# A two-layer mixer and mixture-of-experts kernel: layer 1's modulation products placed in layer 0's merge, and half of layer 0's slot-token groups placed in the expert steps

## The reference

```python
mod = silu(c or c_ctx) @ w_mod[l] + b_mod[l]      # 6 x 1024: shift, scale, gate, twice
h   = rms_norm(x) * (1 + scale) + shift
p   = h @ w_in[l]                                 # q k v, pool, hyena, 3 x 1024 gates
y0, y1, y2 = neighbourhood_attention, multiscale_pool, hyena
x  += gate * (sum_n sigmoid(gates_n) * (y_n @ w_branch[l, n])) @ w_out[l]
h   = modulated rms_norm(x)
# router: 16 experts in 4 groups, best group, top 2 of it
out = sum_e gates[:, e] * ((silu(h @ w_gate[e]) * (h @ w_up[e])) @ w_down[e])
x  += gate * out
```

## Time and profile before

| What | Value |
|---|---|
| Median of 3 runs | 1738.56 us (1735.78 to 1742.26) |
| The profiled execution, its own time | 1740.76 us |
| Its span in the trace | 1739.0 us |
| PE busy | 1495.9 us (86%) |
| DVE busy | 850.8 us (49%) |
| ACT busy | 635.6 us (37%) |
| POOL busy | 368.8 us (21%) |
| DMA, mean over the span | 215 GB/s |

### The profile page before, as it was taken

The page is one execution under the profiler, slowest core; times in us unless marked ns, Lnnn a source line. Parts: engine busy times, 40 slices in busy tenths (PEclk is TensorE's granted clock), DMA queues, the critical chain, the costliest instruction groups (busy, mean ns, idle before and its releaser), DMA issues. The chain is left out here.

```text
span 1739.0 us, 19624 instructions
## 1 busy us (share of the span) xinstructions
PE 1495.9 (86%) x7748; PEld 1076.0 (62%) x7748; DVE 850.8 (49%) x1204; ACT 635.6 (37%) x848; POOL 368.8 (21%) x206
## 2 busy tenths in 40 slices
PE   6998998789999977999999787679889986977772
PEld 2465677568788746788888535468679973322322
DVE  4621765762223246899999556144764633100002
ACT  2422222372232242778777434223164441000003
POOL 0223222112233301111010122335226631000001
PEclk8999999899999986999999888889899997999996
DMA  8457221102232315899999772752314657999992
GB/s 298 170 194 274 74 73 49 36 11 73 92 126 72 121 32 226 343 401 406 406 400 400 252 262 85 294 202 97 100 43 152 206 203 293 420 420 423 422 375 85
DMA packets 120003, 374.32 MB, mean 215 GB/s; under 512 B 8270, under 2 KB 74000, under 8 KB 88944
## 3 DMA queue, kind: packets, MB, share of 16 engines
q1 hardware_dynamic: 109168, 334.58, 51.0%
q0 software_dynamic: 10752, 38.61, 5.9%
HBM read 356.39 MB, written 16.78 MB: 215 GB/s over the span
## 5 line engine op out<-in xcount | busy, mean ns | idle before, releaser
L658 POOL TENSOR_TENSOR w_lo<-ring,w_hi 128x1024 fp32r<-128x1024 f32 x120 | 299.2, 2503 | 629.3 <-ACT w_hi L1431 629.2
L775 PE MATMUL bank<-h_hi,w_hi 128*128 128x512 f32 (+1 forms) x768 | 272.1, 354 | 15.5 <-DVE h_lo L1753 10.8
L776 PE MATMUL bank<-h_hi,w_lo 128*128 128x512 f32 (+1 forms) x768 | 265.2, 345 | 0.0
L777 PE MATMUL bank<-h_lo,w_hi 128*128 128x512 f32 (+1 forms) x768 | 264.7, 345 | 0.0
L775 PEld LDWEIGHTS bank<-h_hi,w_hi 128*128 128x128 f32 x768 | 148.6, 194 | 53.4 <-issue 27.4
L776 PEld LDWEIGHTS bank<-h_hi,w_lo 128*128 128x128 f32 x768 | 149.1, 194 | 16.8 <-issue 1.2
L777 PEld LDWEIGHTS bank<-h_lo,w_hi 128*128 128x128 f32 x768 | 148.7, 194 | 16.9
L775 PE MATMUL bank<-w_hi,h_hi 128*128 128x512 f32 (+1 forms) x384 | 142.5, 371 | 9.9 <-DVE w_lo L2058 5.1
L1431 ACT ACTIVATE w_hi<-ring 128x1024 fp32r<-128x1024 f32 x120 | 125.3, 1053 | 63.3 <-DMA ring<-in_w_in 34.2
L777 PE MATMUL bank<-w_lo,h_hi 128*128 128x512 f32 (+1 forms) x384 | 139.3, 363 | 0.0
L776 PE MATMUL bank<-w_hi,h_lo 128*128 128x512 f32 (+1 forms) x384 | 138.9, 362 | 0.0
(11 more groups left out here) (284 smaller groups left out, 2891.3 us busy)
## 6 DMA issues: line engine op xcount, KB each, us to landing
ring<-in_w_in SPq DMA_DIRECT2D x52, 1024.0 KB, 5.1
ring<-in_w_up_e SPq DMA_DIRECT2D x52, 1024.0 KB, 8.7
mix<-in_w_gate_e SPq DMA_DIRECT2D x51, 1024.0 KB, 8.2
ring<-in_w_mod SPq DMA_DIRECT2D x48, 1024.0 KB, 7.3
operands_plain<-in_w_down_e SPq DMA_DIRECT2D x29, 1024.0 KB, 25.8
mix<-in_w_down_e SPq DMA_DIRECT2D x20, 1024.0 KB, 8.0
ring<-in_w_down_e SPq DMA_DIRECT2D x15, 1024.0 KB, 7.1
y_rows<-mix POOLq DMA_DIRECT2D x24, 512.0 KB, 8.1
```

What stands on the lines that cost most here:

```text
L658: pool.tensor_tensor(w_lo[:, slot], rview(raw, 8)[:, :, x * P:(x + 1) * P], w_hi[:, slot].bitcast(F32), ALU.subtract).then_inc(w_l, 1)
L775: first = mm(dst, stat[0], mov[0], start=start, stop=False)
L776: mm(dst, stat[1], mov[0], start=False, stop=False)
L777: return first, mm(dst, stat[0], mov[1], start=False, stop=stop)
```

## The change

Layer 1's 24 modulation pieces leave the ring. They are loaded one after the other into a buffer of their own, `mod_next`, of one piece; the load of piece p waits until PE has used piece p - 1 (`m_us`). SP issues them between layer 0's merge chunks (`mod_behind`). PE uses one piece after each of the 24 merge tiles of layer 0; the transposes follow two tiles into the next branch, or after the third output tile. PE's loop over n is written out in both layers (`for n in range(3)`). Values of layer 1 go to `mods_next`.

`mod_next` lies where the router weights lay, so `wrt` is loaded after the output projection, ahead of `iota`, on POOL's queue, and PE's router product waits for both.

In layer 0 the slot tokens of groups 8 to 15 move into the expert steps: PE's `slot_tokens(s + 8)` after `rows_t(s + 1)`, DVE's `token_index(s + 8, 1)` after `rows_in(s + 1)`, `slot_one_hot(s + 9)` at the end of step s. The 20 small DVE operations become `shares()`, called in step 0 before `silu(0)`, in both layers.

```diff
-            if l + 1 < DEPTH:
-                order += [("mod", l + 1, k) for k in range(DK)]
...
+            def mod_piece(p):
+                if p:
+                    sp.wait_ge(m_us, p)
+                else:
+                    sp.wait_ge(a_o[0], len(units_of[0]))
+                i, k = divmod(p, DK)
+                sp.dma_start(mod_next, a["w_mod"][1, k * P:(k + 1) * P, i * RW:(i + 1) * RW]).then_inc(s_lds, 16)
+            mod_behind = {at_of[("merge", 0, 0)] + 6 * n + i: [8 * n + k for k in ks] for n in range(3)
+                          for i, ks in ((2, (0,)), (3, (1, 2, 3)), (5, (4,)), (6, (5, 6, 7)))}
...
-                    if at == lo + RS:
+                    if at == lo + RS * (1 - l):
                         filter_transforms(l)
...
-                pool.dma_start(wrt, a["w_router"]).then_inc(r_ld[l], 16)
...
                 pool.wait_ge(o_d[l], 16 * l + 8 * streams(l))
+                pool.dma_start(wrt, a["w_router"]).then_inc(q_io[l], 16)
                 pool.dma_start(iota, a["iota"]).then_inc(q_io[l], 16)
...
-                    if g in MOD_AFTER:
+                    if l == 0 and g in MOD_AFTER:
...
-                with pe.Fori(0, 3) as n:
+                for n in range(3):
...
+                        if l == 0:
+                            mod(1, n, m)
+                            if n and m == 2:
+                                mod_columns(1, n - 1)
...
+                    if l == 0 and m == 2:
+                        mod_columns(1, 2)
...
+                pe.wait_ge(q_io[l], 32 * (l + 1))
                 for k in range(DK):
                     pe.wait_ge(n_h, (2 * l + 1) * DK + k + 1)
...
-                for b in range(NS):
+                for b in range(8):
                     slot_tokens(b)
...
                     if s + 1 < NS:
                         rows_t(s + 1)
+                    if s + 8 < NS:
+                        slot_tokens(s + 8)
...
                     filter_in(l + 1, 0)
-                    mods_and_filters(l + 1, range(DK))
+                    filter_in(l + 1, 1)
+                    filters(l + 1, 0)
+                    spectra_a(l + 1, 0)
+                    spectra_b(l + 1, 0)
                     pe.wait_ge(f_a[l + 1], 6 * l + 10)
-                    pe.wait_ge(m_tk[l + 1], 3 * l + 4)
...
+                        if s == 0:
+                            shares()
+                            if NS > 8:
+                                slot_one_hot(8)
                         silu(s)
...
+                        if s + 8 < NS:
+                            token_index(s + 8, 1)
...
+                    if s + 9 < NS:
+                        slot_one_hot(s + 9)
```

More of the change, by code:

```diff
@@ L276, in build @@
                    for i in range(8)]
+        one_hot += [mix_r[:, 2048 + 512 * i:2560 + 512 * i].rearrange("p (j r) -> p j r", j=4) for i in range(4)]
         fa = area(0, 4096).rearrange("p (j d) -> p j d", j=4)
@@ L616, in _ @@
                     sp.dma_start(rview(at % RS, k), src).then_inc(ring_full[at % RS], 16)
+                    for p in mod_behind.get(at, []):
+                        mod_piece(p)
                 for c in range(EXP_C):
@@ L782, in mod_columns @@
                 for x in range(4):
-                    last = tp(mbank(i)[:, x * P:(x + 1) * P], mrow[:, i % 2, x * P:(x + 1) * P], ident)
+                    rows = mrow_next if l else mrow[:, i % 2]
+                    last = tp(mbank(i)[:, x * P:(x + 1) * P], rows[:, x * P:(x + 1) * P], ident)
                 last.then_inc(m_co[l], 1)
@@ L943, in _ @@
                             mod(l, 1 + i, k + h)
-                    if g in MOD_COLS:
+                    if l == 0 and g in MOD_COLS:
                         mod_columns(l, MOD_COLS[g])
@@ L1381, in mod_rows @@
             def mod_rows(l, i):
+                if l:
+                    act.wait_ge(m_us, DK * (i + 1))
+                    if i:
+                        act.wait_ge(m_co[l], 3 * l + i)
+                    A(mrow_next, mbank(i)[:, :], ACT.Copy).then_inc(m_ev[l], 1)
+                    return
                 act.wait_ge(ring_used, direct_to[at_of[("mod", l, DK * i + DK - 1)]])
@@ L1460, in _ @@
                         spectrum_b(l, 1)
-                    if g in (7, 11):
+                    if l == 0 and g in (7, 11):
                         mod_rows(l, g // 7 if g == 7 else 2)
@@ L1591, in _ @@
                             parts_in(n + 1)
+                        if l == 0 and n and m == 0:
+                            mod_rows(1, n - 1)
                 lead_merged(DK - 1)
                 for m in range(AHEAD, DK):
+                    if l == 0 and m == AHEAD:
+                        mod_rows(1, 2)
                     at = at_of[("out", l, m // 2)]
@@ L1757, in mod_take @@
                 dve.wait_ge(m_co[l], 3 * l + i + 1)
+                if l:
+                    for s in range(2 if i == 0 else 1):
+                        last = V.tensor_tensor(mod_of(l, 16 * i, 16, s).rearrange("p (c x) -> p x c", c=4),
+                                               mbank(i)[:, :].rearrange("p (x c y) -> p x c y", x=4, c=4)[:, :, :, s],
+                                               par[l][:, C_BMOD + 16 * i:C_BMOD + 16 * i + 16]
+                                               .rearrange("p (c x) -> p x c", c=4), ALU.add)
+                    last.then_inc(m_tk[l], 1)
+                    return
                 V.tensor_tensor(mods[:, 16 * i:16 * i + 16, :].rearrange("p (c x) s -> p x c s", c=4),
@@ L1763, in gains @@
             def gains(l, w):
-                for s in range(2):
-                    last = V.scalar_tensor_tensor(gs[:, w, :, s], mods[:, (3 * w + 1) * DK:(3 * w + 2) * DK, s], 1.0,
+                for s in range(2 if l == 0 or w == 0 else 1):
+                    last = V.scalar_tensor_tensor(gs[:, w, :, s], mod_of(l, (3 * w + 1) * DK, DK, s), 1.0,
                                                   par[l][:, C_G1 + 8 * w:C_G1 + 8 * w + 8], ALU.add, ALU.mult)
@@ L1861, in _ @@
                         gate_scales(l, 1)
-                    if g == 9:
+                    if l == 0 and g == 9:
                         mod_take(l, 1)
-                mod_take(l, 2)
+                if l == 0:
+                    mod_take(l, 2)
                 dve.wait_ge(m_tk[l], 3 * l + 3)
                 gains(l, 1)
-                V.tensor_scalar(half_gate[:], mods[:, 2 * DK:3 * DK, :], 0.5, None, ALU.mult).then_inc(m_d[l], 1)
+                for s in range(S):
+                    last = V.tensor_scalar(half_gate[:, :, s], mod_of(l, 2 * DK, DK, s), 0.5, None, ALU.mult)
+                last.then_inc(m_d[l], 1)
                 link(V.memset(up[:, :, 0:POOL_PAD], 0.0))
@@ L2041, in _ @@
                             parts_in(n + 1)
+                        if l == 0 and n and m == 3:
+                            mod_take(1, n - 1)
                 trail_merged(DK - 1)
@@ L2049, in _ @@
                                                ALU.mult, ALU.add).then_inc(o_d[l], 1)
+                    if l == 0 and m == 3:
+                        mod_take(1, 2)
                 dve.wait_ge(o_d[l], 16 * l + 8 * S)
```

141 lines of the change are left out of this document (79 added, 62 removed).

## The result

The changed kernel took 1719.41 us (median of 4 runs, 1716.19 to 1721.18) where the kernel before took 1737.17 (4 runs, 1734.64 to 1742.26): ratio 0.988, 95% interval 0.9861 to 0.99. The forecast was 1719.4. The profiled execution took 1720.27 us, with a span of 1718.5.

What follows compares the result with a forecast made beforehand. PE bound layer 0's merge with DMA free; in layer 1's projection PE waited for w_mod loads. Terms 24.8 - 1.0 - 2.1 - 41.9 + 1.0 = -19.2 us gave 1721.6 profiled, 1719.4 median; range 1711 to 1731.

Steps and rivals of the forecast that it cites:

- Merge, +24.8: Layer 0's merge: 24 pieces at 1.0 us, 1.5 us of transposes, 0.7 us of idle time back; +24.8 us.
- The cover of 2.9 us: Layer 0's merge: 8.4 us tile less 5.1 us landing and 0.4 us issue leaves 2.9 us for a piece's load.
- Into the experts, -1.0: Layer 0's experts: -7.0 us ahead of the first row transposes, +2.0 and +4.0 behind them; sum -1.0 us.
- The -7.0 ahead: Before layer 0's first row transposes: fewer slot groups ahead, until the gather is late next; -7.0 us.
- the 4.0 for eight groups: Layer 0's expert steps: eight moved slot groups cost PE 0.5 us each; +4.0 us.
- The price in the steps: Layer 0's expert steps: +2.0 us for small DVE operations and a one-hot, +4.0 us for eight groups.
- The shares' +2.0: Layer 0's experts: 20 small DVE operations and one one-hot before hidden(0) make it 2.0 us late.
- Between the layers, -2.1: Last expert product to L1318: 4.1 us saved, less 2 us for L824's first part at the lower clock; -2.1 us.
- The 3.3 us for the pieces, the copy and the transposes: Between the layers, behind L824: two pieces 1.9, ACT copy with waits 0.9, four transposes 0.5 us, all leaving.
- the third rival: Between the layers: half clock makes L824, Nyquist products, L837 and spectra_b twice as long; +8 us, 1727; chance 0.11.
- Layer 1's projection, -41.9: Layer 1's projection, tiles 2 to 12: 79.7 us become 37.8, without waits, pieces, transposes and slow clock; -41.9 us.
- Layer 1's router product, +1.0: Layer 1 router: wrt ahead of iota on POOL's queue sends iota some 0.9 us later; +1.0 us.

Runs made afterwards that it cites:

- the run with one copy more: Changed kernel with one 1 MB DRAM-to-DRAM copy on SP's queue ahead of each merge piece's load; ratio 0.9916 of the kernel before.
- the run with the gather first: Changed kernel with four expert loads held until layer 0's first gather landed, and the shares ahead of the rows' copy on DVE; 1712.44 us, ratio 0.9821.
- the slot part alone: Kernel before with only the slot tokens of eight groups and the shares moved, modulation left in place; 1739.18 us, ratio 0.9983.
- the waits filled: Changed kernel with 49 filling products, into a bank nobody reads, in PE's waits between the layers; 1710.55 us, ratio 0.9818.
- the modulation moved alone: Changed kernel with slot tokens and shares put back where the kernel before had them; 1719.84 us, ratio 0.9875.
- the hybrid: Changed kernel with the first eight modulation pieces back between the layers and sixteen in the merge; 1711.01 us, ratio 0.9806.
- resident table: Kernel before with layer 1's last sixteen modulation pieces multiplying a resident table, their w_mod loads left out; ratio 0.9863.

## Why the prediction was right, point by point

- **Merge, +24.8: measured +24.9.** A piece took 1.06 us in its slot instead of 1.0, the transposes 0.5 each as said. 24 x 1.06 + 1.5 is 26.9; PE's gaps at the ends of the loop's rounds, which are gone (three, 2.2 us in all), and shorter waits gave 2.0 back where I took 0.7 and called 1.7 the most that could come back: I had read the idle time of 19 tiles, which doesn't hold all three gaps. Pieces that were 1.4 us too cheap and gaps that were 1.3 too small cancelled; that the sum was right to 0.1 us is luck. The cover of 2.9 us for the loads was the right size: the run with one copy more shows PE waiting 0.4 us a piece once a load lands after 8.3 us.
- **Into the experts, -1.0: measured -2.0.** The -7.0 ahead (measured -7.1) and the 4.0 for eight groups were right; the gather was late next, which the run with the gather first shows by removing its cause. The price in the steps, forecast at +6.0, came out at +5.1 here and with the slot part alone, and at 6.1 and 6.7 between the kernels with the modulation moved. The shares' +2.0 is right within that spread.
- **Between the layers, -2.1: measured -0.6.** Here two terms were mis-sized, the second and most of the first by the clock. I took 0.8 us for an earlier start of L857; it came 10.3 us behind the last expert product instead of 10.4. L846 took 0.5 us more at the lower level, and one DVE operation of the chain behind it 0.54 us instead of 0.28, for which no run here shows a cause. And I took 2 us for a first part of L866 at the lower level; it ran at it for nearly all of its 6.54 us, 2.8 more than L824, on top of the 7.19 that L857 took as before. The 3.3 us for the pieces, the copy and the transposes behind L824 were right: from there to L1318 it is 16.0 us before and 15.5 now, with the 2.8 in it. Of the third rival only the first product came true: L866 ran at half clock, the Nyquist products, L879 and `spectra_b` (3.68 us) did not. That the clock is what L866 lost by is shown: with the waits filled, the same products take 3.70 us and the stretch 32.4.
- **Layer 1's projection, -41.9: measured -42.2.** The sum was made from the price of a full tile, and that held (37.5 us for the stretch, forecast 37.8). The split into 18 us of waits, about 20 of pieces and transposes and the rest clock is confirmed but for the sizes: 25.7 us for waits and clock together, 16.5 for pieces and transposes.
- **Layer 1's router product, +1.0: measured 0.** The wait is there, 0.8 us longer, but only 0.3 of it was left at the product's end, and none at the first gather. The wait for the `h_rows` stores is no cover for it, since the stores follow the product; they too went out 0.3 us later. Why the last 0.3 is gone at the gather (10.2 us from the last store's issue to it, before 10.5) isn't shown.
- **What the sum did not hold:** +1.2 us between norm and ranks and -1.7 us in layer 1 behind the projection. In the kernel with the modulation moved alone the first is +1.1 too, in the hybrid it is 0.0; nothing in the edits touches it, and L1119's product took 9.9 instead of 8.8 us. It isn't the change: the run with 49 fillers has the changed kernel's code there and took 26.5 us, with 9.0 for the product. The granted clock rose from 0.50 to 1.00 some 5.8 us into the product in the changed kernel and 4.0 us into it in that run; why it rises when it does, no run here isolates. The -1.7 lies within what the code of before does by itself: from the first L951 of layer 1 to the end of its norm sums that code took 261.0, 259.1 and 257.4 us in three traces (before, resident table, slot part alone), and the changed kernel 259.6.

The rule of the Trainium skill that I weighed (TensorE: Matmul & The Clock Gate, Part 1: "the default state is throttled, and activity releases the throttle") named what my sum had too small between the layers, and alone it would have been further off: all of these products at the lower level were the third rival's +8 us on my sum, +5.9 for the stretch, where -0.6 was measured. By that rule, the trace agrees in part: thinned out, L857 and L866 ran at 0.50, and with the waits filled at 1.00. Against it, L815 ran at 0.50 in the kernel before as well, at 9.86 of 10 us busy.

## What to carry to other kernels

Before moving work out of a stage where an engine waits, split the stage's time into waits and work, best by running it once with the operand resident: only the waits are won, and the work is merely carried to where it may cost its full price. Work that sits in another engine's shadow (here eight pieces between the layers) is best left there. And when one transfer is late next, look at what runs beside it; here, holding back 4 MB for some 6 us was worth more than the reordering that had exposed the gather.

## What the hardware showed that I had not expected

- The clock in a stretch of thin work isn't fixed by the program. The kernel before and the kernel with the slot part alone issue the same instructions between the layers, and their first filter product took 7.19 us in one (and in the run with the resident table) and, here, 3.70 in the other. From the last expert product to L1318's place that made 38.1 and 38.2 us against 35.5:

```profile
997.32 3.70 PE L825 MATMUL bank<-mix 64*128 64x512 f32 x8 [0.25 <-ACT mix L1405]
```

- The profiled executions reached layer 0's merge between 374.5 and 380.1 us, with the same program up to there. The two rows below (the run with the gather first, then the changed kernel again) have 1680 matmuls each and clocks of 0.95 and 0.93. Effects of a few microseconds must be read from their own stage.

```profile
0.00:374.50 374.50, 319.33 (x1680) 218.66 (x1681) 208.15 (x386) 116.39 (x228) 76.66 (x40) 0.95 0.38 134
```

```profile
0.00:378.70 378.70, 322.76 (x1680) 222.17 (x1680) 211.89 (x386) 116.36 (x228) 77.65 (x40) 0.93 0.38 132
```

- Two gathers of 128 rows, issued 1.5 us apart, landed after 4.4 and 5.8 us by themselves and after 9.0 and 11.9 beside 4 MB of loads, although these were issued on another queue.
